# Four RMS norms around the FFNs, the projections and the output: weight first, root behind the products

## What is computed

```
def rms_norm(x, g):
    y = xf * lax.rsqrt(jnp.mean(xf * xf, axis=-1, keepdims=True) + EPS)
    return y * g
layer 0:  x += hgrn_mixer(rms_norm(x, norm_mix[0]));  x += conv_ffn(rms_norm(x, norm_ffn[0]))
layer 1:  x += dsa_mixer(rms_norm(x, norm_mix[1]));   x += conv_ffn(rms_norm(x, norm_ffn[1]))
y = rms_norm(x, norm_final)
conv_ffn(h):  a, u = split(h @ w_in);  c = conv_b + sum_j shift(a, j) * conv_w[j]
              return (silu(c) * u) @ w_down, last rows of a
dsa_mixer(h): q, k, v, qi, ki, wi = split(h @ w_in); rope on q, k, qi, layer_norm then rope on ki; ...
```

## Time and profile before

| | us |
|---|---|
| median of 3 runs (lowest to highest) | 4141.31 (4141.2 to 4144.04) |
| the profiled execution's own time | 4141.06 |
| its span | 4139.4 |
| TensorE matmuls busy in the span | 3771.9 |
| VectorE, ScalarE, GpSimd busy | 2154.6, 1095.1, 230.6 |

### The profile page before, as it was taken

How to read it: one execution, slowest core, us unless ns; L and a number is a source line. 1 busy time by engine, 2 the same in 40 slices (tenths; PEclk the granted TensorE clock), 3 DMA queues, 4 the chain that set the end, 5 groups by cost and what they waited for, 6 DMA issues and landing times. The chain is left out here.

```text
span 4139.4 us, 55965 instructions
## 1 busy us (share of the span) xinstructions
PE 3771.9 (91%) x19881; PEld 3306.2 (80%) x19897; DVE 2154.6 (52%) x3919; ACT 1095.1 (26%) x1897; POOL 230.6 (6%) x356
## 2 busy tenths in 40 slices
PE   6999999996999999998978699887889799999997
PEld 5988898885999999987975245553459699999997
DVE  5455555545444444445458867775323444444445
ACT  4322233223111111122223244342331321111111
POOL 2000000003000000002000010000000300000000
PEclk8888888878999999999985856677999999999999
DMA  2111111000111111111120200002321111111111
GB/s 84 35 35 34 38 37 38 27 21 31 39 44 47 39 42 46 37 45 59 63 88 21 66 12 10 6 1 79 143 111 41 33 46 47 37 45 45 40 41 58
DMA packets 58111, 187.23 MB, mean 45 GB/s; under 512 B 6985, under 2 KB 23377, under 8 KB 53521
## 3 DMA queue, kind: packets, MB, share of 16 engines
q1 hardware_dynamic: 53216, 165.23, 11.8%
q0 software_dynamic: 4656, 18.65, 1.4%
HBM read 164.28 MB, written 19.57 MB: 44 GB/s over the span
## 5 line engine op out<-in xcount | busy, mean ns | idle before, releaser
L206 PE MATMUL ff1lin<-ff1h_hi,ff1w_hi 128*128 128x384 f32 x1056 | 355.7, 337 | 24.0 <-POOL ff1h_lo L164 15.6
L206 PE MATMUL ff0lin<-ff0h_hi,ff0w_hi 128*128 128x384 f32 x1056 | 356.2, 337 | 22.0 <-POOL ff0h_lo L164 14.2
L207 PE MATMUL ff0lin<-ff0h_lo,ff0w_hi 128*128 128x384 f32 x1056 | 355.4, 337 | 0.0
L208 PE MATMUL ff0lin<-ff0h_hi,ff0w_lo 128*128 128x384 f32 x1056 | 355.1, 336 | 0.0
L208 PE MATMUL ff1lin<-ff1h_hi,ff1w_lo 128*128 128x384 f32 x1056 | 354.8, 336 | 0.0
L207 PE MATMUL ff1lin<-ff1h_lo,ff1w_hi 128*128 128x384 f32 x1056 | 354.7, 336 | 0.0
L206 PE MATMUL hg_lin<-hg_h_hi,hg_w_hi 128*128 128x384 f32 x768 | 270.5, 352 | 16.3 <-POOL hg_h_lo L164 14.4
L207 PE MATMUL hg_lin<-hg_h_lo,hg_w_hi 128*128 128x384 f32 x768 | 264.5, 344 | 0.0
L208 PE MATMUL hg_lin<-hg_h_hi,hg_w_lo 128*128 128x384 f32 x768 | 264.1, 344 | 0.0
L206 PEld LDWEIGHTS ff1lin<-ff1h_hi,ff1w_hi 128*128 128x128 f32 x1056 | 200.0, 189 | 26.5 <-POOL ff1h_lo L164 16.2
L206 PEld LDWEIGHTS ff0lin<-ff0h_hi,ff0w_hi 128*128 128x128 f32 x1056 | 200.3, 190 | 24.5 <-POOL ff0h_lo L164 14.9
(11 more groups left out here) (348 smaller groups left out, 8163.7 us busy)
## 6 DMA issues: line engine op xcount, KB each, us to landing
ff0raw<-in_weights SPq DMA_DIRECT2D x66, 512.0 KB, 3.6
ff1raw<-in_weights SPq DMA_DIRECT2D x66, 512.0 KB, 3.6
hg_raw<-in_weights SPq DMA_DIRECT2D x40, 512.0 KB, 3.6
as_keys<-in_cache_k SPq DMA_DIRECT2D x16, 1024.0 KB, 4.8
as_vals<-in_cache_v SPq DMA_DIRECT2D x8, 2048.0 KB, 9.2
pj_raw<-in_weights SPq DMA_DIRECT2D x18, 512.0 KB, 4.3
se_keys<-in_cache_ki SPq DMA_DIRECT2D x8, 1024.0 KB, 4.9
x<-in_x SPq DMA_DIRECT2D x3, 1536.0 KB, 8.7
```

The source lines that it names most:

```text
L206: pe.matmul(out, w_hi, x_hi, start=start, stop=False)
L207: pe.matmul(out, w_hi, x_lo, start=False, stop=False)
L208: return pe.matmul(out, w_lo, x_hi, start=False, stop=stop)
```

## The change

1. **Squares early.** In the stage in front of a changed norm, ScalarE squares each block of x as soon as its last addition is done; GpSimd adds the squares of the channel blocks (9 additions in the mixer stage, 18 in the others), and the remaining blocks go to TensorE directly: 15 sums in the first FFN, 6 in the others, instead of 24.
2. **First two raw slabs early.** The SyncE queue loads them at the end of the stage in front, as soon as the raw buffers (or their place) are free.
3. **Products without the root.** `h_hi` is the rounded x * gain, made by ScalarE from x; `h_lo` is (x * gain) - `h_hi`, made by VectorE in one instruction per block. GpSimd no longer takes part, but splits slab 1. TensorE waits for each block of the first slab rather than for a group.
4. **The root behind.** In the FFN VectorE, not ScalarE, takes the gate rows out of PSUM, times the root; and it multiplies the silu's result by the root before the up rows. In the projections cos and sin are multiplied by the root once; the indexer key is multiplied before its layer norm; for token-wise rows TensorE turns the root (9 transposes) and ScalarE takes it as a per-partition scale, one instruction per 128 frames instead of 384.
5. **Also.** y is made where `y_lo` will stand; the final stage keeps three y buffers and stores each group in two halves; one DMA at the start brings all five gains, instead of one per norm.

Cut to its core:

```diff
+class Ahead:
+    def square(self, act, x, nb, g):
+        m = (nb - 1) * G + g
+        if m >= self.slots:
+            act.wait_ge(self.pooled, m - self.slots + 1)
+        act.activation(self.place(nb, g), x[:, nb, g * GT:(g + 1) * GT], ACT.Square).then_inc(self.squared, 1)
+    def add_squares(self, pool):
+        for nb in range(1, self.direct):
+            for g in range(G):
+                pool.wait_ge(self.squared, nb * G + g + 1)
...
+                pool.tensor_tensor(self.acc[:, g], self.acc[:, g], self.place(nb, g), ALU.add).then_inc(self.pooled, 1)
+    def sums(self, pe, ones, banks):
+        pe.wait_ge(self.squared, KB * G)
+        pe.wait_ge(self.pooled, (self.direct - 1) * G)
+        for g in range(G):
+            pe.matmul(banks[g][:, 0:GT], ones[:, :], self.acc[:, g], start=True, stop=False)
+            for nb in range(self.direct, KB):
+                i = pe.matmul(banks[g][:, 0:GT], ones[:, :], self.place(nb, g), start=False, stop=nb == KB - 1)
+            i.then_inc(self.summed, 1)
+class Scaled:
+    def low(self, dve, g):
+        for kb in range(KB):
+            dve.wait_ge(self.a.hi_done, g * KB + kb + 1)
+            dve.scalar_tensor_tensor(self.h_lo[:, kb, g * GT:(g + 1) * GT], self.x[:, kb, g * GT:(g + 1) * GT],
+                                     self.gain[:, kb:kb + 1], self.h_hi[:, kb, g * GT:(g + 1) * GT].bitcast(F32),
+                                     ALU.mult, ALU.subtract).then_inc(self.a.lo_done, 1)
+    def first_block(self, pe, W, out, slot, g):
+        for kb in range(KB):
+            pe.wait_ge(self.a.lo_done, g * KB + kb + 1)
...
 hgrn_phase
+        later = Ahead(nc, env, "ff0", env["ffn_first"][0], t_at["hg_raw"], acc_at=env["ff_y_hi"], sq_at=env["ff_a_ext"],
+                      slots=12, direct=4)
             over_bodies(act, body)
+            for nb in range(KB):
+                for g in range(G):
+                    act.wait_ge(dve_evac, ADDED + nb * G + g + 1)
+                    later.square(act, x, nb, g)
 ffn_phase, ScalarE
-            N.on_scalar(act, lambda: W.split_hi(act, 0, 0, 0, 0, 0))
+            hi(0, 0)
+            N.high(act, 0)
+            hi(0, 1)
+            for g in range(G):
+                ahead.root(act, std, lin[G:], g)
+            N.high(act, 1)
+            N.high(act, 2)
 ffn_phase, VectorE
-            N.on_vector(dve, lambda: W.split_lo(dve, 0, 0, 0))
+            W.split_lo(dve, 0, slot(0, 0), 0)
+            for g in range(G):
+                N.low(dve, g)
+            for g in range(G):
+                ahead.invert(dve, std, g)
...
+            def gate_rows(c, j):
...
+                    last = dve.tensor_tensor(a_ext[:, j, W_EXT + a:W_EXT + b], lin[g][:, 0:b - a], std[:, g, 0:b - a], ALU.mult)
             def up_rows(c, par, j):
                 hold(dve, silu_done, blk + 1, tk)
+                dve.tensor_tensor(conv[:, j], conv[:, j], rstd, ALU.mult)
 project_phase, VectorE
+            dve.tensor_tensor(cos_r[:, :], cos[:, :], rstd, ALU.mult)
+            dve.tensor_tensor(sin_r[:, :], sin[:, :], rstd, ALU.mult)
 project_phase, ScalarE
-                        act.activation(wi[:, 3 * g:3 * g + 3, :], lin[g][:, 0:GT].rearrange("p (t c) -> p t c", c=P)[:, :, 0:IDX_H],
-                                       ACT.Copy, scale=WI_SCALE).then_inc(evac, 1)
+                        for tile in range(3 * g, 3 * g + 3):
+                            i = act.activation(wi[:, tile, :], lin[g][:, tile % 3 * P:tile % 3 * P + IDX_H], ACT.Copy,
+                                               scale=rt[:, 1, tile, 0:1])
program
+                sp.dma_start(gains[:, :, :], io["gains"].rearrange("n p k -> p n k")).then_inc(consts_in, 16)
+                sp.wait_ge(consts_in, 16 * (len(const) + 1))
```

More of the change, by code:

```diff
@@ new lines, with __init__, high @@
+class Scaled:
+    def __init__(self, ahead, x, gain, h_hi, h_lo):
+        self.a, self.x, self.gain, self.h_hi, self.h_lo = ahead, x, gain, h_hi, h_lo
+    def high(self, act, g):
+        for kb in range(KB):
+            act.activation(self.h_hi[:, kb, g * GT:(g + 1) * GT], self.x[:, kb, g * GT:(g + 1) * GT], ACT.Copy,
+                           scale=self.gain[:, kb:kb + 1]).then_inc(self.a.hi_done, 1)
+    def low(self, dve, g):
[5 more added lines that the diff above has]
+    def first_block(self, pe, W, out, slot, g):
+        for kb in range(KB):
+            pe.wait_ge(self.a.lo_done, g * KB + kb + 1)
+            last = W.product(pe, out, slot, kb * P, self.h_hi[:, kb, g * GT:(g + 1) * GT],
+                             self.h_lo[:, kb, g * GT:(g + 1) * GT], kb == 0, kb == KB - 1)
+        return last
@@ L180, in load_all @@
     def load_all(self, sp):
-        for s in range(2):
+        for s in range(0 if self.ahead else 2):
             sp.dma_start(self.raw[:, s], self.weights[self.first + s]).then_inc(self.loaded[s], 16)
@@ L329, in _ @@
             W.load_all(sp)
+            for k in range(2):
+                sp.wait_ge(W.lo_done, 39 + k)
+                later.load(sp, io["weights"], k)
         @block.gpsimd
@@ L812, in _ @@
             sp.dma_start(conv_p[:, :, :], io["conv_p"][layer]).then_inc(consts_in, 16)
-            sp.dma_start(gain[:, :], io["gains"][env["ffn_gain"][layer]]).then_inc(consts_in, 16)
             W.load_all(sp)
             if layer == 0:
+                sp.wait_ge(W.units, units_before(CHUNKS - 1) + 12)
+                for k in range(2):
+                    later.load(sp, io["weights"], k)
                 for spent in env["spent"]:
@@ L888, in body @@
                     return
[L889 to L890 removed]
+                if not (isinstance(c, int) and c == 0):
+                    hi(c, 1)
                 hi(c, 2)
@@ L903, in _ @@
             over_chunks(act, body)
+            for nb in range(KB):
+                for g in range(G):
+                    act.wait_ge(down_out, ADDED + nb * G + g + 1)
+                    later.square(act, x, nb, g)
         @block.vector
@@ L1137, in _ @@
         def _(sp):
-            for dst, src in ((cos[:, :], io["cos"]), (sin[:, :], io["sin"]), (ln[:, :], io["ki_ln"]), (gain[:, :], io["gains"][2])):
+            for dst, src in ((cos[:, :], io["cos"]), (sin[:, :], io["sin"]), (ln[:, :], io["ki_ln"])):
                 sp.dma_start(dst, src).then_inc(consts_in, 16)
@@ L2088, in _, with squares @@
             W.load_all(sp)
+            for k in range(2):
+                sp.wait_ge(W.lo_done, KB - 1 + k)
+                later.load(sp, io["weights"], k)
+        @block.gpsimd
+        def _(pool):
+            later.add_squares(pool)
         @block.scalar
         def _(act):
+            def squares(nb):
+                for g in range(G):
+                    act.wait_ge(added, G * nb + g + 1)
+                    later.square(act, x, nb, g)
             for g in range(G):
```

280 lines of the change are left out of this document (179 added, 101 removed).

## The result

The changed kernel took 4035.62 us (median of four executions, 4034.03 to 4039.03) against 4141.31: ratio 0.9744, interval 0.9727 to 0.9761. The forecast was 4042, 4032 to 4060. The profiled execution took 4034.98, its span is 4033.4.

The account below looks back on a forecast made before the run. TensorE bounds the middle of stages; only the norm heads and last norm can shorten. Savings 33.2 + 32.4 + 29.5 (heads) + 5.8 (end) - 1.4 (start) = 99.5; 4141.3 - 99.5 = 4041.8, rounded 4042 us, range 4032 to 4060.

Parts of the forecast that it names:

- The heads: Stage starts at a norm: savings of 33.2 us in the second FFN, 32.4 in the first, 29.5 net in the projections.
- third slab: Third weight slab's first matmul, marking a head's end: about T0 + 35 (first FFN, projections), T0 + 33 (second FFN).
- a low part every 0.54: VectorE in the heads: each two-input low part of 384 columns takes 0.54 us, as in the final norm.
- fifteen sums ... 9.9, they end at 973.3: First FFN's head: fifteen TensorE sums at 0.66 us take 9.9; both slabs' products then end at 998.3.
- I take 1.8 here too: Second FFN's head: TensorE's 2.0 us wait costs 1.8 more at the 1.2 GHz level, leaving 33.2 saved.
- clock loss 1.8 again: Projections' head: TensorE waits 4.2 us and loses 1.8 more to the lower clock.
- The sentence that I set beside the row: Second FFN's head: the clock falls back only in waits longer than 2.0 us, so 35.0 would be saved; not adopted.
- 0.27 apart, five times that: Kernel start: the DMA of all gains, five times 128 short pieces, loses 1.4 us.
- The stores: Final norm: the last store moves 768 KB instead of 1536 KB, saving 1.8 us, between nothing and 3.0.
- The indexer's and the values' copies: Projections: nine indexer weight copies instead of three add 1.4 us; the values' copies, three for one, add 0.6.
- What cost nothing: Chunks stay 76.4 us, VectorE about 41 busy; GpSimd keeps up at 0.99 per addition; additions to x stay 0.55.
- The sum: Whole kernel: 33.2 + 32.4 + 29.5 + 5.8 - 1.4 = 99.5 us saved, giving 4042.

Follow-up runs that it names:

- the new order on VectorE: Changed kernel with ScalarE's high parts all ahead of the roots, VectorE making slab 1's low part, 12 sums in the first FFN: 4036.04 us; with 15 sums, 4033.18.
- the second measurement: The changed kernel measured once more, unedited: 4038.78 us against 4141.19, ratio 0.9754 (0.9741 to 0.9767).

## Why the prediction was right

*The heads.* Right, and nearly to the figure: third slab forecast 33.5 behind the last addition in the second FFN (33.55), 35.7 in the projections (35.47), 35.9 in the first FFN (37.95). What sets it was named rightly: VectorE in the first two, TensorE's sums in the third. The runs show both: shorter sums moved the first FFN's head alone, the new order on VectorE the other two. Of the 98.8 that the three heads gained, the early slabs (14.6), the FFNs' early squares (14.0) and the order on VectorE (25 to 27) were each taken away and measured. The rest was not: above all that VectorE makes a low part every 0.54 in one instruction, where its product took 1.35 and GpSimd's low part 1.31, stands on the rows alone.

*The first FFN's 2 us.* The step "fifteen sums ... 9.9, they end at 973.3" was mis-sized: it took full clock from the first sum on and the stage's end right behind the last square. The trace shows 1.7 for the clock and 0.5 for GpSimd's late end.

*The clock losses.* "I take 1.8 here too" and "clock loss 1.8 again" were wrong in the profiled execution: behind 1.63 in the second FFN and 2.58 in the projections (forecast 4.2; nine transposes stand in front of that one) products ran on at full clock. In other runs the wait at this place in the projections (2.0 to 2.6) was followed by no matmul at the 0.32 spacing or by nine to eleven. The size of this term is not fixed by the wait. The sentence that I set beside the row, from the Trainium skill (TensorE: Matmul & The Clock Gate, section "HAM oscillation — how this bites in real kernels"), agrees with 1.63 and not with the 2.5 us waits that did cost something. That the rests still lost about what was forecast is luck: in the projections 1.7 went at a wait for which the forecast has no clock term (next paragraph), in the second FFN 2.2 went at the three waits of "issue".

*Start and end.* The gains' DMA cost 0.12 to 0.29 in ten profiles, 0.24 in the changed kernel's, not 1.4; the step "0.27 apart, five times that" took landings in turn for a price. The stores gave 2.6, not 1.8, so the end 6.5.

*The indexer's and the values' copies.* Forecast 2.0, of which 1.4 on the indexer's path: mis-sized. ScalarE, then TensorE, before and now:

```profile
1971.57 0.19 ACT L1193 ACTIVATE at_wi<-pj_lin 128x24 f32<-128x24 f32 x1 [0.28 <-PE pj_lin L1295]
...
1972.86 2.20 PE L1301 MATMUL pj_ln<-pj_swapped,c_ones_v 128*128 128x384 f32 x6 [1.33 <-ACT pj_swapped L1196]
```

```profile
1903.30 1.52 ACT L1338 ACTIVATE at_wi<-pj_lin,pj_rt 128x8 f32<-128x8 f32 x9
...
1905.92 3.90 PE L1459 MATMUL pj_ln<-pj_swapped,c_ones_v 128*128 128x384 f32 x6 [1.92 <-ACT pj_swapped L1342]
```

Nine copies take 1.52 where three took 0.93 (from 1970.83 to 1971.76), and TensorE's wait grew from 1.33 to 1.92: 0.6, in all nine executions with the copies. The values' copies add 0.7 at two places, and the stage's last wait is 0.3 shorter: 0.9 together, not 2.0. The six matmuls behind the 1.92 took 3.90 instead of 2.20, at the lower clock; these 1.7 and the 0.9 are the 2.6 of the table. The rest of the projections was 233.7 and 233.8 on two executions without the copies and 233.4 to 237.8 on nine with them; that spread is mostly such clock losses, so the totals don't show the price of the copies.

*What cost nothing.* Held: additions to x, GpSimd's pace, and the chunks, but for the three waits of "issue" in the second FFN.

*The sum.* The heads and the end gave 105.3 against 106.5 in the forecast. The 106.0 of the profiled execution are these 105.3 and 4.3 up to the mixer's end, less 3.5 in all the rests. The 4.3 is the mixer's spread and not a gain: the second measurement gives 102.4 between the medians. That the first median lay closer to the range's low end than to 4042 was not the change's doing.

## What to carry to other kernels

Where stages begin with a norm, look at the head alone, from the last instruction in front of it to the point where the old order runs again: each engine's chain there, added up from rows of the same shapes, gave the new length within half a microsecond in two cases of three. Multiplying a row-wise root in behind the product pays by what it lets the matrix engine start early (25 to 27 us here), not by saved work. Judge by stretches of the trace when wholes spread by more than the edit is worth, and count the helper engine's way to the end of a stage, not only its last instruction.

## What the runs showed of the hardware

- GpSimd's last addition was followed by the next stage 2.31 and 2.32 us later where it ended late, while ScalarE's last square was followed 0.3 later where GpSimd's last addition had ended 2.3 or more ahead of that stage. What fills the 2.3 is not shown.
- The same wait of 2.47 us in front of the last chunk's down product was followed by none or by seven to eleven matmuls at the 1.2 GHz spacing (0.32 instead of 0.173), in the two executions of the changed kernel as well: up to 1.6 us that the length of the wait does not decide.
- The mixer, with the same work on TensorE and VectorE, took from 956.9 to 962.8 us over the profiled executions, and selection with attention from 962.6 to 968.0.
